# Second block's attention: where the second projection quarter of a step stands against the transposes

## The reference

```
proj = h @ w_in[l]
q, k, v, f_logit, cx, cb, cc, px, gate_logit = jnp.split(proj, IN_SPLITS, axis=-1)
...
for i in range(S // Q_BLOCK):
    logits = jnp.einsum('bhqd,bhkd->bhqk', qb, kb) * scale
    logits = logits + (c[:, :, q0:q1, None] - c[:, :, None, :q1])
    logits = jnp.where(causal, logits, -jnp.inf)
    p = jax.nn.softmax(logits, axis=-1)
    outs.append(jnp.einsum('bhqk,bhkd->bhqd', p.astype(vb.dtype), vb))
```

## Time and profile before

| what | value |
|---|---|
| median of 3 runs (lowest, highest) | 3135.59 us (3134.44, 3141.13) |
| the profiled execution: its own time | 3134.47 us |
| its span, first to last instruction | 3132.7 us |
| PE busy, share of the span | 99% |
| DVE, ACT, POOL busy | 50%, 34%, 8% |
| mean granted TensorE clock | 0.997 |
| one attention stage, from S(0) to the end of PV(17) | 140.8 us, twice |

### The profile page before, as it was taken

The page is one execution under the profiler, slowest core; times in us unless marked ns, Lnnn a source line. Parts: engine busy times, 40 slices in busy tenths (PEclk is TensorE's granted clock), DMA queues, the critical chain, the costliest instruction groups (busy, mean ns, idle before and its releaser), DMA issues.

```text
span 3132.7 us, 38793 instructions
## 1 busy us (share of the span) xinstructions
PE 3101.5 (99%) x15548; PEld 2594.6 (83%) x15548; DVE 1575.0 (50%) x1897; ACT 1076.0 (34%) x1169; POOL 237.5 (8%) x139
## 2 busy tenths in 40 slices
PE   9999999999999999999999999999999999999998
PEld 7798988888889798888888778888888878888887
DVE  7564545554335654555435764544434766444433
ACT  3223334443222443444323332333323332333322
POOL 0002100010000020010000000111000000100100
PEclk9999999999999999999999999999999999999999
DMA  4411412222331131222223122222222322222223
GB/s 170 114 55 68 148 41 94 94 98 103 115 114 68 45 145 55 81 94 103 99 108 115 56 93 99 91 102 94 98 108 89 95 81 99 91 95 105 94 107 108
DMA packets 47723, 299.94 MB, mean 96 GB/s; under 512 B 7091, under 2 KB 7347, under 8 KB 13284
## 3 DMA queue, kind: packets, MB, share of 16 engines
q1 hardware_dynamic: 42480, 288.01, 25.7%
q10 hardware_dynamic: 5108, 10.02, 1.4%
HBM read 293.26 MB, written 4.75 MB: 95 GB/s over the span
## 4 chain that ended last, share of the span: by engine, by line
PE 91%; DVE 5%; ACT 2%; issue 2%; DMA 0%; DVEq 0%; ACTq 0%; POOL 0%; SPq 0%
PE G L444 83%; ACT wH L1217 1%; DVE wL L1638 1%; PE psS L794 1%; DVE mxt L1846 1%; PE psS L504 1%; PE psS L995 0%; PE psS L1096 0%; PE G L1105 0%; PE G L1002 0%; DVE ws L2410 0%; PE psT L536 0%; PE psT L1132 0%; PE G L1020 0%; DVE ws L2229 0%
## 5 line engine op out<-in xcount | busy, mean ns | idle before, releaser
L444 PE MATMUL G<-hH,wH 128*128 128x512 f32 x2560 | 1017.4, 397 | 7.7 <-DVE wL L1638 3.3
L444 PE MATMUL G<-hH,wL 128*128 128x512 f32 x2560 | 999.3, 390 | 0.0
L444 PE MATMUL G<-hL,wH 128*128 128x512 f32 x2560 | 998.8, 390 | 0.0
L1638 DVE TENSOR_TENSOR wL<-raw,wH 128x2048 fp32r<-128x2048 f32 x264 | 635.2, 2406 | 640.2 <-ACT wH L1217 639.8
L444 PE MATMUL G<-wsr,wH 128*128 128x512 f32 (+1 forms) x2512 | 744.7, 380 | 1.4 <-DVE wsr L2245 0.9
L1217 ACT ACTIVATE wH<-raw 128x2048 fp32r<-128x2048 f32 x265 | 505.5, 1907 | 578.0 <-PE G L444 558.1
L444 PEld LDWEIGHTS G<-hH,wH 128*128 128x128 f32 x2560 | 481.7, 188 | 122.8 <-issue 18.7
L444 PEld LDWEIGHTS G<-hH,wL 128*128 128x128 f32 x2560 | 481.7, 188 | 102.8
L444 PEld LDWEIGHTS G<-hL,wH 128*128 128x128 f32 x2560 | 482.2, 188 | 99.2 <-issue 2.2
L444 PEld LDWEIGHTS G<-wsr,wH 128*128 128x128 f32 x2512 | 463.4, 188 | 92.1 <-DVE wsr L2245 1.8
L444 PE MATMUL G<-wsr,wL 128*128 128x512 f32 (+1 forms) x1256 | 475.8, 379 | 0.0
(11 more groups left out here) (290 smaller groups left out, 2521.3 us busy)
## 6 DMA issues: line engine op xcount, KB each, us to landing
raw<-in_units SPq DMA_DIRECT2D x265, 1024.0 KB, 4.8
ws<-bias_rows SPq DMA_DIRECT2D x2, 1536.0 KB, 14.9
bias_rows<-ws ACTq DMA_DIRECT2D x1, 2560.0 KB
x<-in_x SPq DMA_DIRECT2D x4, 512.0 KB, 7.5
ws<-in_mem ACTq DMA_DIRECT2D x2, 1024.0 KB, 4.8
ws<-bias_rows ACTq DMA_DIRECT2D x1, 2048.0 KB, 8.5
out_x<-x SPq DMA_DIRECT2D x4, 512.0 KB, 7.5
ws<-in_decay ACTq DMA_DIRECT2D x1, 1280.0 KB, 8.5
```

The lines of the kernel that those rows point to most:

```text
L444: mm = pe.matmul(o, mv if swap else wt, wt if swap else mv, start=first and n == 0, stop=last and n == 2)
L1638: V.tensor_tensor(wL[:, g.p, :], raw[:, g.p, :], wH[:, g.p, :].bitcast(F32), ALU.subtract)\
```

## The change

The second quarter of a step, Q2(d), moves ahead of the transposes T(d). The norm products that stood behind Q2(d) stay where they were, behind T(d) and ahead of PV(d). To do that, the function `fill` is cut in two. What is computed doesn't change, and no semaphore wait is added or taken away.

```
                         value_quarter(s_ % 4)
                     elif s_ < 36:
                         quarter(s_ % 4)
+
+                def norms(s_):
+
                     if s_ == 5:
...
                     fill(2 * d)
+                    fill(2 * d + 1)
                     if 1 <= d <= 16:
                         for r in (2 * d - 2, 2 * d - 1):
...
                             mm.then_inc(t_done, 1)
-                    fill(2 * d + 1)
+                    norms(2 * d + 1)
                     if d == 7:
                         values = c.job.v + 2
```

## The result

The changed kernel takes 3176.11 us (median of 4 runs, 3174.56 to 3178.91), the kernel before on the same chip 3137.07 (4 runs, 3134.44 to 3141.13): 39.0 us more, a ratio of 1.0128 with a 95% interval from 1.0116 to 1.014. The forecast was 3165 with a range up to 3176: direction and place were right, the size was too small by 11 us, and the time lies 0.1 us above the range. Of the 11 us 2.6 are the base, since the forecast started from the profiled execution's 3134.47 and not from the median; as a difference, 30.6 us were forecast and 39.0 measured.

A forecast was written before the change was run, and what follows sets the result against it. PE's own list was taken to set the time, with next to no waiting to win back. Added waits of 7.8 and 7.5 us, 15.3 a layer and 30.6 for two, on 3134.47 gave 3165 us, range 3150 to 3176.

The forecast's parts named there:

- The early half: Steps 1 to 6 of each layer: waits that follow the later transposes delay PE by 7.8 us a layer.
- job release: Steps 1 and 3: the next Q1 waits for DVE's reading of a job, 0.9 and 1.1 us.
- first sums: Step 2, sums of squares: PE waits 1.1 us for ACT's square, which stands behind the copies.
- second sums: Step 6, sums of squares behind the heads' output: PE waits 1.86 us for DVE's low part.
- The spread's term: Step 4 into 5, spread of columns: late by T(4)'s whole shift, so the delay grows from 3.1 to 5.9 us.
- The late half: Steps 8 to 16: cycles of two steps through DVE's job reading grow by 1.45 and 2.3 us, together 7.5 a layer.
- The waits' sum: Both attention stages: 7.8 plus 7.5 gives 15.3 us of delay a layer, 30.6 for two.
- The clock falls: Rival, chance 0.04: each layer's two longest waits halve PE's clock for one quarter, 2.8 us each; 11 us, 3176.
- Borders: Changes between kinds of matmul on PE: a gain of near nothing, at most 5 us over both layers.
- More: Rival, chance 0.10: each late pair of steps costs 2.3 us, first half 9; 3171, or 3176 with a late weight unit.
- Not slower: Rival, chance 0.05: ACT's copies stay held by the exponentials, so only borders count; 3129 to 3135 us.
- Only the first half: Rival, chance 0.08: steps 1 to 6 cost 7.8 us a layer, DVE's cycle from step 8 stays hidden; 3150 us.

The follow-up runs named there:

- e1: Changed kernel with ACT's copies out of psT put behind the step's square, heads' output and weight rounding (steps 1 to 15): 3133.84 us, ratio 0.9991.
- e9: As e3, but with 16 and 24 transposes ahead of the two groups of sums of squares, leaving no wait there: 3169.65 us, ratio 1.0105.
- e2: Kernel before, PE's order old, with only the move in ACT's list that e1 makes: 3135.22 us, ratio 0.9997.
- e3: Changed kernel plus 108 unread transposes a layer on PE, filling most of each wait: 3170.78 us, ratio 1.0107.
- e5: Old order of the kernel before in steps 0 to 6, changed order from step 7 on: 3152.25 us, ratio 1.0055.
- e6: As e1, but steps 2 and 6 keep the old order, with the quarter between transposes and sums of squares: 3133.87 us, ratio 0.9994.
- e7: As e3, but 4 and 7 unread matmuls of 512 columns ahead of the two groups of sums replace 8 and 15 transposes: 3170.85 us, ratio 1.0109.
- e8: As e7, but with 9 and 13 wide matmuls ahead of the two groups of sums, so no wait is left there: 3170.33 us, ratio 1.0109.
- e4: Changed order in steps 0 to 6 alone, old order of the kernel before from step 7 on: 3163.27 us, ratio 1.0081.

## Why the prediction was off in size

- **What bounds the kernel, and the mechanism: right.** T releases the copies; T of 4 to the copies took 0.42 us, as worked out. e1 shows that ACT's order is the cause.
- **The early half: right.** Predicted and measured waits: job release in steps 2 and 4 0.9 and 0.88, 1.1 and 0.99; first sums 1.1 and 1.02; second sums 1.86 and 1.89. The spread's term, a delay growing by 2.8, shows as 2.39 at the spread and 0.23 at Q1(5). That each release was followed through ACT's list and set against PE's remaining work is what made these good to 0.2.
- **The late half: right in sum.** T(8) to T(10) 17.23 us against 17.3. T(10) to T(12) 19.46 in the first stage, where the clock fell behind Q1(12), and 17.92 in the second, where it did not, against 18.0. T(12) to T(14) and T(14) to T(16) grew by 1.3 and 2.2 us against 1.45 and 2.3. The prediction had put the whole wait on Q1(10), Q1(12), Q1(14) and Q1(16); Q1(11) and Q1(15) waited too, 0.98 us each, and line 1099 0.2 to 0.4 in steps 10, 12 and 14.
- **The waits' sum: right.** 15.3 us a layer predicted; 15.1 by the estimate from e9, 14.3 by PE's idle time.
- **The rival "The clock falls": the step that failed.** It was given 0.04, and set up as an alternative to the forecast. It was a term that comes on top of the waits. The sum of 3165 thus held nothing for the clock, and the prediction's own sign of being wrong, a clock under 1.00, came: 0.95 and 0.97 in the two stages. The ground for the 0.04 was that a 1.4 us wait in the first block left no mark in the clock's slices. But a slice is 78 us long there, and a drop of a few microseconds does not show in a tenth of it: the same trace has one, behind 32 matmuls of one column (line 495), that the earlier trace rows does not show. And one execution was not enough: behind that same 1.4 us wait the clock stayed up in the profile before, and fell in those of e2, e3, e5 and e9. The lines are the stretch around the wait and the one behind line 495 in the kernel before, and the stretch around the wait in e9:

```profile
1036.00:1046.00 10.00, 8.17 (x50) 6.34 (x49) 8.55 (x21) 4.41 (x14) 0.00 (x0) 1.00 0.55 212
1074.50:1079.50 5.00, 5.00 (x17) 3.95 (x18) 2.36 (x2) 2.28 (x2) 0.25 (x1) 0.66 0.00 0
...
1036.00:1046.00 10.00, 8.27 (x39) 5.87 (x39) 8.59 (x19) 4.48 (x15) 0.00 (x0) 0.83 0.55 211
```

The rival's price came near by luck. It had four drops, at the spread and the second sums of each layer, of 2.8 us each, 11 us in all; about 9 were measured by medians. The profiled execution has seven, four in one stage and three in the other, also at the first sums and at Q1(12), and they cost 14.2 us of PE's busy time (8.6 and 5.6), 2.0 each. So there were more of them, and each was cheaper. The sum should have been 3165 plus that term, 3176, with room above.
- **Borders: right.** e1 against e2 differs in PE's order alone, with no waits left: 139.63 to 140.02 us in the first stages, 0.4 us over 16 steps, 0.02 a step. The medians, 3133.84 and 3135.22, are too close to tell.
- **The other rivals fell.** "More" also ended at 3176 (3134.5 + 42.0, rounded down), but by other means: each layer would have waited 18.2 us and 2.8 more for a weight unit, where PE's idle time grew by 14.3 and no weight unit (line 1642) held PE in the stages. "Not slower" needed the copies to be held longer than T's shift: ACT's 2.44 us of idle time shows T holding them. "Only the first half": e5 has the second half alone, at 1.0055.

## What to carry to other kernels

Before a producer is moved later in one engine's list, read the in-order list of the engine that consumes it: what stands behind the consumer is moved too, whether or not it needs the producer. Here 15 us a layer went that way, and putting the consumer behind the independent work took all of it back without touching the change. Where PE ran at a granted clock of 1.00 and is given waits, add a term for the clock on top of them, and look for earlier drops in stretches of a few microseconds, not in slices of the whole span, and in more than one execution. The version with both edits, e1, has the lowest median of all (3133.84; e6 3133.87), but its 0.9991 [0.9982, 1.0] is no gain that can be told from none.

## What the runs showed of the hardware

**Short waits can cost the clock.** Drops to the lower level came with waits of 1.02, 1.67, 1.89 and 2.39 us, and with waits of only 0.09 to 0.28 us ahead of the sums of line 507 (3 of 4 groups in e3, 4 of 4 in e7). With the wait ahead of the sums filled completely none came in the profiles (e8, e9, 0 of 8). The Trainium skill, TensorE: Matmul & The Clock Gate, section A second HAM failure mode: psum-queue depth-cycling, tells of a kernel whose short idle times between groups of matmuls made the gate go back and forth; the traces here agree, with 0.58 to 0.78 in the stretches behind the waits.

**And not each time.** The same 1.67 us wait of Q1(12) had a drop in one stage of the changed kernel and none in the other; e4 likewise in its early waits. The 28 waits of 0.88 to 1.33 us ahead of the other quarters, in the profiles of the changed kernel, e4 and e5, had none. So the length of the wait alone does not decide.

**A wait is not needed either.** In 3 of 28 groups of sums in the seven profiles that have no wait ahead of them (before, e1, e2, e5, e6, e8, e9) a drop came with no idle time in front. One such drop is worth about 1.5 us (the 141.12 us of e1's second stage against 139.63). Behind the 32 matmuls of one column of line 495, which take 3.63 us and stand ahead of the attention stages, the clock fell in all eleven profiles with no idle time (0.66 in the stretch of the kernel before that is shown above). What decides at the sums stays open, and so does why 0.09 to 0.28 us ahead of them was enough, where the 0.17 us left ahead of e3's spread was not.

**ACT works strictly in its order.** It stood idle for 2.44 us ahead of copies, with a square and a rounding behind them that did not need T: in e1 they began at 1714.26 and 1714.74. The Trainium skill, TensorE: Matmul & The Clock Gate, section Architectural detail: the array is 16× 32×32, not 1× 128×128, says the same of ACT and DVE, that they are strict queues; e1 shows what that was worth here, some 42 us between the medians of the two kernels.
